# Expert gather and combination in a mixture-of-experts step: one fp32 product in place of three bf16 parts

## The reference

```python
# x: 256 tokens x 1024;  64 experts, 6 chosen per token, expert width 256
scores = sigmoid(x @ w_router)
eidx   = top_k(group_limited(scores + router_bias), 6)
wsel   = scores[eidx] / sum(scores[eidx]) * 2.5
combine = one_hot(eidx) weighted by wsel            # 256 x 64
hid    = silu(x @ w_gate[e]) * (x @ w_up[e])        # for each expert e
routed = sum_e (hid * combine[:, e]) @ w_down[e]
out    = routed + (silu(x @ ws_gate) * (x @ ws_up)) @ ws_down
```

## Time and profile before

| | |
|---|---|
| median of 3 runs | 1532.53 us (1530.97 to 1533.79) |
| the profiled execution, its own time | 1534.29 us |
| its span | 1532.5 us |
| PE busy | 1485.4 us |
| PEld busy | 1056.8 us |
| DVE busy | 461.1 us |
| ACT busy | 440.1 us |
| mean granted TensorE clock | 0.989 |

### The profile page before, as it was taken

The page is one execution under the profiler, slowest core; times in us unless marked ns, Lnnn a source line. Parts: engine busy times, 40 slices in busy tenths (PEclk is TensorE's granted clock), DMA queues, the critical chain, the costliest instruction groups (busy, mean ns, idle before and its releaser), DMA issues.

```text
span 1532.5 us, 30939 instructions
## 1 busy us (share of the span) xinstructions
PE 1485.4 (97%) x13231; PEld 1056.8 (69%) x13231; DVE 461.1 (30%) x949; ACT 440.1 (29%) x1093; POOL 3.2 (0%) x17
## 2 busy tenths in 40 slices
PE   5999999999999999999998999999999999999996
PEld 3868779676666767666666859676767666676764
DVE  2244441622222222222223251612222222222224
ACT  2124331323232232322222131422222323222233
POOL 0000000000000000000000000000000000000000
PEclk8999999999999999999999999999999999999997
DMA  9976679489999999999999038469999999999970
GB/s 354 395 271 223 231 275 350 190 334 395 407 386 409 399 405 391 400 399 411 395 394 275 20 124 342 193 240 398 386 407 392 410 396 396 405 393 398 402 306 29
DMA packets 101443, 510.55 MB, mean 333 GB/s; under 512 B 11256, under 2 KB 19600, under 8 KB 52240
## 3 DMA queue, kind: packets, MB, share of 16 engines
q1 hardware_dynamic: 97440, 506.57, 83.7%
q10 hardware_dynamic: 3952, 3.24, 0.6%
HBM read 506.65 MB, written 3.15 MB: 333 GB/s over the span
## 4 chain that ended last, share of the span: by engine, by line
PE 94%; ACT 2%; DVE 2%; DMA 1%; SPq 1%; issue 0%; DVEq 0%; ACTq 0%
PE psum L1288 91%; PE psum L1617 1%; DMA arena<-in_ada_w 1%; ACT arena L543 1%; SPq L388 1%; DVE arena L840 0%; ACT arena L566 0%; PE psum L1499 0%; PE psum L1740 0%; PE psum L1784 0%; DVE arena L842 0%; DVE arena L1181 0%; DVE arena L1177 0%; ACT L554 0%; PE psum L1412 0%
## 5 line engine op out<-in xcount | busy, mean ns | idle before, releaser
L1288 PE MATMUL psum<-arena 128*64 128x256 f32 (+9 forms) x12948 | 1454.9, 335 | 25.5 <-DVE arena L1181 6.8
L1288 PEld LDWEIGHTS psum<-arena 128*64 128x64 f32 (+3 forms) x12948 | 1026.8, 135 | 447.6 <-issue 235.0
L543 ACT ACTIVATE arena<-psum 128x192 f32<-128x192 f32 (+5 forms) x550 | 198.3, 387 | 381.3 <-PE psum L1288 317.9
L1177 DVE TENSOR_TENSOR arena<-psum,arena 128x512 f32<-128x512 f32 x128 | 88.1, 688 | 315.8 <-ACT arena L543 315.8
L543 ACT ACTIVATE arena<-arena 128x512 bf16<-128x512 f32 (+1 forms) x144 | 87.5, 618 | 111.5 <-DVE arena L1177 108.9
L1181 DVE TENSOR_TENSOR arena<-arena 128x512 bf16<-128x512 f32 x128 | 88.7, 693 | 98.0 <-ACT arena L543 98.0
L705 ACT ACTIVATE arena<-psum 128x256 f32<-128x256 f32 x64 | 24.6, 385 | 299.1 <-PE psum L1288 299.1
L1170 DVE SCALAR_TENSOR_TENSOR arena<-arena,psum 128x256 f32<-128x256 f32 x64 | 30.8, 481 | 262.0 <-ACT arena L705 262.0
L1160 DVE COPY arena<-psum 128x192 f32<-128x192 f32 x128 | 39.8, 353 | 95.8 <-PE psum L1288 95.8
L885 DVE SCALAR_TENSOR_TENSOR arena<-psum,arena 128x128 f32<-128x128 f32 x64 | 18.0, 344 | 63.3 <-PE psum L1288 63.3
L550 ACT ACTIVATE arena<-arena 128x512 f32<-128x512 f32 x20 | 12.3, 629 | 73.2 <-DVE arena L885 72.2
(11 more groups left out here) (142 smaller groups left out, 288.1 us busy)
## 6 DMA issues: line engine op xcount, KB each, us to landing
arena<-in_moe_w_gate SPq DMA_DIRECT2D x64, 2048.0 KB, 9.6
arena<-in_moe_w_up SPq DMA_DIRECT2D x64, 2048.0 KB, 14.1
arena<-in_moe_w_down SPq DMA_DIRECT2D x64, 2048.0 KB, 10.9
arena<-in_ada_w SPq DMA_DIRECT2D x24, 2048.0 KB, 12.6
arena<-in_hgrn_w_in SPq DMA_DIRECT2D x10, 2048.0 KB, 13.7
arena<-in_na_w_qkv SPq DMA_DIRECT2D x6, 2048.0 KB, 17.4
arena<-in_hgrn_w_out SPq DMA_DIRECT2D x1, 4096.0 KB, 13.6
arena<-in_na_w_o SPq DMA_DIRECT2D x1, 4096.0 KB, 13.9
```

The source lines that it names most:

```text
L543: return act.activation(out, in_, ACT.Copy, **kw)
L1177: dve.tensor_tensor(y_rest[:, at], psum[:, 6 + half, :], y[:, j, 0, at], ALU.subtract)\
L1288: return pe.matmul(out, lhsT, rhs, start=start, stop=stop, skip_group_check=True, **kw)
```

## The change

The token rows `h_tok` are kept once, in fp32, and the gather is one fp32 product where it was three bf16 products. The results `y` are kept once, in fp32 and in one buffer; the combination is one fp32 product where it was three. The one-hot matrix is made a second time, in fp32, for the gather (`hots32`); the bf16 one stays for `turn_hots`. The turned one is fp32. The splits on ACT and DVE are gone: ACT copies the first half of the results, DVE the second, with the features stored so that the stationary blocks are contiguous. The gather waits for these two copies in place of the subtractions, the combination waits for them too. In the front, ACT copies the token rows after the routing scores, not before. The last combination of a pass moves from behind the passes into the pass.

```diff
-        h_tok = sc(3 * D, (3, 2, K, P), BF16)
+        h_tok = sc(2 * D, (2, K, P))
+        hots32 = sc(2 * 2 * 2 * SLOTS, (2, 2, 2 * SLOTS))
-        onehot_t = sc(2 * P, (2, 2, P), BF16)
+        onehot_t = sc(2 * NT, (2, NT))
-        y = sc(3 * D, (2, 3, D), BF16)
+        y = sc(D)
...
+        def token_bank(n):
+            return (h_tok[:, n % 2, 4 * (n // 2):4 * (n // 2 + 1)],
+                    psum[:, n, :].rearrange("p (k q) -> p k q", q=P))
+
+        def result_bank(half):
+            return (y.rearrange("p (k q) -> p k q", k=K)[:, :, 64 * half:64 * (half + 1)],
+                    psum[:, 6 + half, :].rearrange("p (q k) -> p k q", k=K))
...
 (POOL, zeroing the gaps between slots)
-                pool.wait_ge(M.h_low, 4)
+                pool.wait_ge(M.htok, 4)
...
 (ACT, experts_front: after the scores' sigmoid, in place of the copies ahead of it and the middle parts)
+                for n in range(4):
+                    act.wait_ge(M.htok_ps, n + 1)
+                    copy(*token_bank(n)).then_inc(M.htok, 1)
...
 (ACT, pair_step)
-                for half in range(2):
-                    act.wait_ge(M.y_ps[half], n + 1)
-                    at = slice(half * BLOCK, (half + 1) * BLOCK)
-                    copy(y[:, j, 0, at], psum[:, 6 + half, :]).then_inc(M.y_high, 1)
-                    act.wait_ge(M.y_rest, n * 2 + (half + 3))
-                    copy(y[:, j, 1, at], y_rest[:, at]).then_inc(M.y_mid, 1)
+                act.wait_ge(M.y_ps[0], n + 1)
+                copy(*result_bank(0)).then_inc(M.y_sb[0], 1)
...
 (DVE, one_hots)
-                dve.tensor_tensor(hots, slots..., ranks..., ALU.is_equal).then_inc(M.onehot, 1)
+                for out in (hots32[:, j].rearrange("p a (e s) -> p a e s", e=2), hots):
+                    ins = dve.tensor_tensor(out, slots..., ranks..., ALU.is_equal)
+                ins.then_inc(M.onehot, 1)
...
 (DVE, experts_front: the four subtractions to h_rest and the four to the low parts are gone)
 (DVE, pair_step: the four subtractions are gone)
+                dve.wait_ge(M.y_ps[1], n + 1)
+                dve.tensor_copy(*result_bank(1)).then_inc(M.y_sb[1], 1)
...
 (PE, gather)
-                    pe.wait_ge(M.y_rest, results * 2 + (half + 1))
+                    elif not unread:
+                        pe.wait_ge(M.y_sb[half], results)
                     for i in range(4):
                         for a in range(2):
-                            for part in range(3):
-                                ins = mm(psum[...], h_tok[:, part, a, 4 * half + i], hots[:, a], ...)
+                            ins = mm(psum[...], h_tok[:, a, 4 * half + i], hots32[:, j, a], a == 0, a == 1)
...
 (PE, combine)
+                for half in range(2):
+                    pe.wait_ge(M.y_sb[half], results)
                 for k in range(K):
-                    for part in range(3):
-                        ins = mm(psum[...], y[:, j, part, k::K], onehot_t[:, j]..., False, False)
+                    ins = mm(psum[...], y[:, k * P:(k + 1) * P], onehot_t[:, j], False, False)
...
 (PE, down)
-                    pe.wait_ge(M.y_low, n)
-                    combine(M, 1 - j)
+                    combine(M, n, 1 - j)
...
 (PE, experts_pass, at its end; the combination behind the passes is gone)
+                combine(M, n0 + PAIRS, 1, last=True)
```

More of the change, by code:

```diff
@@ L469, in _ @@
             load_stage(qkv0 + 2)
-            sp.wait_ge(moe[0].done, 4)
+            sp.wait_ge(moe[0].done, more * 4 + 4)
             sp.dma_start(ck, io["cache_na_k"][0, 0].rearrange("s h d -> s (h d)")).then_inc(cache_in, 16)
@@ L671, in experts_front @@
                 act.activation(lb_t[:, 0:1], eps, ACT.Sigmoid)
[L672 to L675, removed]
                 act.wait_ge(M.logits, 1)
@@ L694, in hots_turned @@
                 act.wait_ge(M.hot_ps, n + 1)
-                copy(onehot_t[:, j].rearrange("p a t -> p (a t)"), psum[:, 5, 0:NT])
+                copy(onehot_t[:, j], psum[:, 5, 0:NT])
                 for e in range(2):
@@ L1071, in one_hots @@
                 ranks = rank[:, :, bass.ds(expert, 2)] if not isinstance(expert, int) else rank[:, :, expert:expert + 2]
-                dve.tensor_tensor(hots, slots.unsqueeze(1).unsqueeze(1).broadcast_to(shape),
-                                  ranks.unsqueeze(3).broadcast_to(shape), ALU.is_equal).then_inc(M.onehot, 1)
+                for out in (hots32[:, j].rearrange("p a (e s) -> p a e s", e=2), hots):
+                    ins = dve.tensor_tensor(out, slots.unsqueeze(1).unsqueeze(1).broadcast_to(shape),
+                                            ranks.unsqueeze(3).broadcast_to(shape), ALU.is_equal)
+                ins.then_inc(M.onehot, 1)
             def experts_front(m):
                 M = moe[m]
-                dve.sem_inc(M.y_rest, 2)
                 normed(2 * m + 1)
@@ L1082, in experts_front @@
                 link(dve.memset(cand, 2 * LOW))
[L1083 to L1087, removed]
                 dve.wait_ge(M.scores, 1)
@@ L1122, in experts_front @@
                 done()
[L1124 to L1129, removed]
                 def shared_hidden(a):
@@ L1204, in added @@
                     if k % 2 == 0:
-                        dve.wait_ge(M.done, k // 2 + 1)
+                        dve.wait_ge(M.done, more * 4 + (k // 2 + 1))
                 residual(mod[:, m, 5], added)
@@ L1555, in shared_down, with gather @@
                 ins.then_inc(M.sh_used, 1)
-            def gather(M, n, results, j, after_shared=False):
-                hots = onehot[:, j].rearrange("p a (e s) -> p a e s", e=2)[:, :, :, 0:SLOTS]
+            def gather(M, n, results, j, after_shared=False, unread=False):
                 pe.wait_ge(M.onehot, n + 1)
@@ L1582, in turn_hots, with combine @@
                 ins.then_inc(M.hot_ps, 1)
-            def combine(M, j, last=False):
+            def combine(M, results, j, last=False):
+                for half in range(2):
+                    pe.wait_ge(M.y_sb[half], results)
                 for k in range(K):
-                    for part in range(3):
-                        ins = mm(psum[:, k // 2, (k % 2) * NT:(k % 2 + 1) * NT], y[:, j, part, k::K],
-                                 onehot_t[:, j].rearrange("p a t -> p (a t)"), False, False)
+                    ins = mm(psum[:, k // 2, (k % 2) * NT:(k % 2 + 1) * NT], y[:, k * P:(k + 1) * P], onehot_t[:, j],
+                             False, False)
                     if last and k % 2:
@@ L1612, in down @@
                 if next_expert is not None:
-                    gather(M, n + 1, n, 1 - j)
+                    gather(M, n + 1, n, 1 - j, unread=first)
                 pe.wait_ge(M.hid, n + 2)
@@ L1648, in experts_pass @@
                     shared_down(M)
-                down(M, n0, 0, load0, 2, first=isinstance(r, int))
+                down(M, n0, 0, load0, 2, first=True)
                 gate_up(M, n0 + 1, 1, load0)
@@ L1661, in experts @@
                 pe.wait_ge(M.gaps, 4)
+                pe.wait_ge(M.htok, 4)
                 experts_pass(M, 0)
@@ L1667, in experts @@
                         experts_pass(M, r + 1)
-                pe.wait_ge(M.y_low, more * PAIRS + PAIRS)
-                combine(M, 1, last=True)
             experts_front(0)
```

25 lines of the change are left out of this document (4 added, 21 removed).

## The result

The changed kernel takes 1675.28 us (median of 4 runs, 1674.57 to 1675.61), the kernel before 1533.16 us on the same chip (4 runs, 1530.97 to 1535.13). The ratio is 1.0927, 95% interval 1.0908 to 1.0946: 142 us slower. The forecast was 1673 us.

What follows compares the result with a forecast made beforehand. PE's instruction stream was taken as the bound. Gather +96.6, combination +50.2 and layer ends -6.2 gave +140.6 us on 1534.3, 1674.9 us; with the median 1.8 us lower, 1673.1 us (+9.2%), range 1652 to 1700.

Steps and rivals of the forecast that it cites:

- PE's stream is the bound, and the copies and splits are hidden: Repeating pairs: PE busy in 456.62 of 456.62 us, so ACT's and DVE's work there costs nothing.
- Gather, +1.51 us a pair: Gather in each pair: 32 fp32 records at 0.112 us, 3.58 us in place of 2.07; +96.6 us over 64 pairs.
- the three prices: Gather record of 96 columns: 0.112 us taken; 0.081 by columns alone, 0.140 with load and columns in series.
- Combination, +0.81 us: Combination in each pair: 16 records at 0.215 us, 3.45 us in place of 2.64; +50.2 us over 62 pairs.
- The strided end: Combination's upper end: 0.024 us more a record as with strided weights, +24 us, 1697 us; inside the forecast's 0.82.
- Pair 18.07 us: Period of one pair of experts in PE's stream: 15.75 + 1.51 + 0.81 us, transfers at 348 GB/s.
- The ends, -3.1 us each: End of each layer's experts: one copy replaces the splits, clock stays full; gain 2.9 to 3.4 us, together -6.2 us.
- Front, nothing: Before the first expert weights: dropped splits and moved token copies are off the path, so no time changes.
- Rival 4: Gather and combination: fp32 products take one record each, 2.0 us less a pair, about 1500 us; chance 0.02.
- the stop by the transfers: Weight transfers in the pairs: already filling 0.99 of a pair, they limit a gain to about 1500 us, otherwise 1400.
- stream +146.8: All pairs in PE's stream: the gather's +96.6 us and the combination's +50.2 us.
- rival 1: Gather: columns set the pace, 0.081 us a record, 63 us less, 1610 us; chance 0.07.

## Why the prediction was right

- **PE's stream is the bound, and the copies and splits are hidden:** the pieces touch each other in before and after, and four copies in place of one left the period as it was.
- **Gather, +1.51 us a pair:** measured +1.52 alone. The choice between the three prices, made because 64 and 128 columns cost the same in the trace, was the decisive one, and the runs with 64 and 128 columns bear it out.
- **Combination, +0.81 us:** measured +0.82 alone; 0.215 us a record, as in the row of contiguous weights. The strided end, put at 24 us, costs 30.
- **Pair 18.07 us:** 18.09 to 18.10. Transfers forecast at 348 GB/s and a share near 0.87: 350 and 0.89.
- **The ends, -3.1 us each:** -3.5. The copy takes 0.69 us, not up to 1.09, so PE waits 0.89 us and not 1.5; the clock kept 2.4 GHz as taken. The path was not quite the one foretold. There DVE's additions set the pace and the root followed the last square as before or sooner. The last square does start 6.29 us after `down` (forecast 7.26), but the root starts 2.80 us after it, where it was 2.50: it waits for PE's sums, which begin only at 884.72, 0.73 us after the combination, and take 3.75 us.
- **Front, nothing:** +0.64 and +1.41 us, with the first gather of each layer (1.52 us) in it, thus -0.9 and -0.1 without.
- **Rival 4** was rightly put aside, since the fp32 products make two records. Its time was mis-sized: it set the stop by the transfers at about 1500 us. Room until 14.91 us a pair brings 1458 to 1460 us, as the kernels with fewer parts show. A transfer share of 0.99 at 399 GB/s was not the end; those kernels reach 421 to 422.

The forecast came out 2.2 us under the median. Nearly all of that is the scatter of executions: the profiled one of before lies 1.1 us over its median, that of after 0.7 us under. By the table its terms compare thus: stream +146.8, measured 142.0 + 4 x 0.82 for the combinations behind it + 2 x 1.52 for the first gathers = 148.3; ends -6.2, measured -7.1; front 0, and 0.64 + 1.41 less the first gathers is -1.0. Together 140.2 of the 140.3 us. That the sum of the forecast (+140.6) fits to 0.3 us is in part luck: the stream was put 1.5 us too low, and the ends and the front together 1.9 us too high.

So the kernel is slower for a reason of counting. A one-hot matrix has no digits to lose, and three bf16 parts hold the fp32 value, so three records suffice. One fp32 product is two records, and each is dearer than a bf16 one: at 96 columns by the weight load (0.112 against 0.043 us), at 256 by the columns (0.215 against 0.110). Two times 0.112 is more than three times 0.043, and two times 0.215 more than three times 0.110. What the change saves lies on engines that nothing waits for, but for the 3.5 us at each layer's end, and those count from an execution of before in which the clock fell at both ends.

The Trainium skill, page FP8 and Floating Point Precision, section TensorE Precision Notes, counts four passes for fp32. The runs agree at 256 columns (two records of 0.215 us, and four times 256 columns at 2.4 GHz are 0.427 us); at 64 to 128 columns the price is another, and the page's count alone would have given 1610 us, by the estimate of rival 1. The Trainium skill, page TensorE: Matmul & The Clock Gate, section LDWEIGHTS, gives columns / 1.2 for a weight load, 107 ns here. The rows have 110 and 113 ns for fp32 weights. For bf16 weights of the same size they have less: 43 ns for a whole record of the old gather.

## What to carry to other kernels

Before parts are merged into one wider product, count records and price each by the larger of weight load and columns, from the narrowest and the widest shape of that type in the trace: a product of few columns is paid by its load. A change that frees engines off the critical path is worth only what the ends of the stream show, and a few microseconds there can be hidden or undone by when the engine's code arrives, so try small end effects at more than one placement. Of the versions tried, two bf16 parts beat both kernels (1459.99 us, 0.9525) at the price of exactness; none that keeps all of it beat before by more than can be measured.

## What was not expected of the hardware

- PE stands idle for 0.42 to 3.41 us between the last fp32 combination and the norm's sums, or in the middle of the sums (2.47 and 2.75 us), and goes on 1.29 to 1.48 us after a 16 KB transfer of instructions on queue 8 has ended. Moving the code by 128 instructions made a hole in the middle of the sums, and moving it by 64 did not.
- One core's weight stream ran at 421 to 422 GB/s over 270 us, though the share already showed 0.99 at 399.
- After waits of 3.06 to 3.64 us the granted clock fell to 1.2 GHz at some layer ends and held 2.4 GHz at others, in two kernels at the two ends of the same execution (3.06 us: fell and held; 3.64 us held and 3.23 us fell). Idle times of 2.75 and 3.41 us in the holes were followed by 1.2 GHz, those of 2.47 and 2.83 us were not. No run here shows what decides.
- Weights of fp32 at a stride of eight elements cost 0.031 us more a record with 256 columns (0.246 against 0.215), though the load lies under the columns when they are contiguous.
- Semaphore increments on PE are not free: PE's first product starts at 6.09 us without them, at 10.71 with 64 and at 20.49 with 128, and of that 1.3 and 3.9 us are left at the second root.
